# Two blocks of a transformer on one core: expert weights through seven and nine buffers in order of use, with the loops over experts written out

## The reference, cut to what matters

```python
def hier_moe(h, wr_g, br_g, wr_e, br_e, w_gate, w_up, w_down):
    p_group = softmax(xf @ wr_g + br_g)            # 4 groups, the best one is taken
    e_val, e_sel = top_k(fine of that group, 2)    # 2 of its 8 experts per token
    gate = p_top * softmax(e_val)
    ...
    y = (silu(x_rows @ w_gate[e]) * (x_rows @ w_up[e])) @ w_down[e]   # for each expert's tokens
    out[token] += y * gate
# layer 0 of the second block: conv_mixers, then hier_moe
# layer 1 of the second block: attn_mixers, then hier_moe, then the final rmsnorm
```

## Time and profile before

| what | value |
|---|---|
| runs | 2086.3, 2087.37, 2092.24 us; median 2087.37 |
| profiled execution | 2085.26 us, of which the span is 2083.3 us |
| TensorE busy | 2004.8 us (96%) |
| VectorE busy | 898.7 us (43%) |
| ScalarE busy | 371.7 us (18%) |
| moved by DMA | 592.64 MB, mean 284 GB/s |
| first expert stage | about 916 to 1390 us of the span |
| second expert stage | about 1598 to 2073 us |

### The profile page before, as it was taken

One profiled execution on the slowest core, in us unless ns is written; L12 is line 12 of the kernel. 1 busy time (PEld: TensorE's weight loads), 2 busy tenths in 40 slices (PEclk: granted clock), 3 DMA queues, 4 the chain that ended last, 5 costly groups with the idle time before them and its releaser, 6 DMA issues.

```text
span 2083.3 us, 21716 instructions
## 1 busy us (share of the span) xinstructions
PE 2004.8 (96%) x8126; PEld 1105.4 (53%) x8126; DVE 898.7 (43%) x1829; ACT 371.7 (18%) x767; POOL 93.0 (4%) x185
## 2 busy tenths in 40 slices
PE   8989999998999999799999999989999999999997
PEld 5556666545666658554443444447765443444442
DVE  3354553245355417856776666662534111011102
ACT  2321000033100010121111111112332111111111
POOL 1111110011111000000000000000000000000000
PEclk9999999999999999999999999999998999999999
DMA  7326885333488742529999999983251999999995
GB/s 265 139 81 245 300 326 222 135 122 121 157 317 313 273 162 81 202 80 416 430 428 429 428 429 428 428 321 122 81 202 41 408 427 428 428 429 428 428 428 249
DMA packets 109523, 592.64 MB, mean 284 GB/s; under 512 B 16663, under 2 KB 21270, under 8 KB 84886
## 3 DMA queue, kind: packets, MB, share of 16 engines
q1 hardware_dynamic: 96406, 541.48, 64.4%
q0 software_dynamic: 13056, 50.33, 6.4%
HBM read 590.74 MB, written 1.05 MB: 284 GB/s over the span
## 4 chain that ended last, share of the span: by engine, by line
PE 81%; DMA 12%; DVE 3%; POOL 1%; issue 1%; ACT 1%; SPq 0%; POOLq 0%; DVEq 0%; ACTq 0%
PE bank L1100 23%; DMA ring<-in_moe_w_up 12%; PE bank L758 11%; PE bank L771 11%; PE bank L982 7%; PE bank L694 6%; PE bank L1084 6%; PE bank L1091 3%; PE bank L895 3%; PE bank L1002 3%; PE bank L806 1%; PE bank L1215 1%; PE bank L1233 1%; PE bank L1262 1%; POOL rstd L619 1%
## 5 line engine op out<-in xcount | busy, mean ns | idle before, releaser
L1100 PE MATMUL bank<-ring,work 128*64 128x512 f32 x3072 | 672.9, 594 | 16.3 <-DMA ring<-in_moe_w_up 16.3
L1100 PEld LDWEIGHTS bank<-ring,work 128*64 128x64 f32 x3072 | 221.3, 137 | 436.2 <-issue 435.7
L2391 DVE SCALAR_TENSOR_TENSOR work<-work 128x512 f32<-128x512 f32 x384 | 258.6, 746 | 5.1 <-DVE work L2388 4.9
L758 PE MATMUL bank<-hT,ring 128*128 128x256 f32 x1024 | 223.5, 380 | 0.7 <-ACT hT L1373 0.7
L771 PE MATMUL bank<-ring,work 128*128 128x512 f32 x512 | 222.5, 593 | 0.0
L758 PEld LDWEIGHTS bank<-hT,ring 128*128 128x128 f32 x1024 | 194.8, 190 | 32.2 <-issue 6.9
L2395 DVE SCALAR_TENSOR_TENSOR work<-work,bank 128x512 f32<-128x512 f32 x32 | 21.9, 686 | 391.8 <-ACT work L1570 391.8
L2120 DVE SCALAR_TENSOR_TENSOR work<-ring,cond,work 128x512 f32<-128x512 f32 x168 | 126.3, 752 | 85.8 <-DMA ring<-in_ada_w 80.5
L771 PEld LDWEIGHTS bank<-ring,work 128*128 128x128 f32 x512 | 97.4, 190 | 115.4 <-issue 114.6
L982 PE MATMUL bank<-hT,ring 128*128 128x256 f32 x608 | 137.3, 388 | 0.3 <-ACT hT L1487 0.3
L694 PE MATMUL bank<-ring,hT 128*128 128x512 f32 (+1 forms) x320 | 135.0, 579 | 0.0
(11 more groups left out here) (384 smaller groups left out, 1517.6 us busy)
## 6 DMA issues: line engine op xcount, KB each, us to landing
ring<-in_moe_w_gate SPq DMA_DIRECT2D x64, 2048.0 KB, 15.4
ring<-in_moe_w_up SPq DMA_DIRECT2D x64, 2048.0 KB, 17.1
ring<-in_moe_w_down SPq DMA_DIRECT2D x64, 2048.0 KB, 12.7
ring<-in_ada_w POOLq DMA_DIRECT2D x48, 1024.0 KB, 9.3
ring<-in_w_up SPq DMA_DIRECT2D x16, 2048.0 KB, 12.8
ring<-in_w_down SPq DMA_DIRECT2D x16, 2048.0 KB, 10.0
ring<-in_w_in SPq DMA_DIRECT2D x10, 2048.0 KB, 8.0
ring<-in_cd_w_in SPq DMA_DIRECT2D x6, 2048.0 KB, 9.1
```

Source lines behind the costliest of these rows:

```text
L758: last = pe.matmul(B(4 + b)[:, (c % 2) * S:(c % 2) * S + S], w[:, k, c * P:c * P + P], hT[:, k, :], start=(k == 0), stop=(k == DT - 1))
L1100: last = pe.matmul(b[h, :], x[:, k, h], w[e][:, k, c0:c0 + 512], start=(k == 0), stop=(k == kk - 1))
L2391: mo.do(dve.scalar_tensor_tensor(fl(bias[:, h]), mask_b, rbt[:, bass.ds(12 * bk + h, 1)], fl(bias[:, h]), ALU.mult, ALU.add))
```

## The change

- **Memory.** A tile `seventh` of one slot is added. It takes the place of small tiles that only the first block and the preparation of the second use (masks, tables, row constants): they are now cut out of it, and it is free for weights in the expert stages. The router's bias gets a tile of its own.
- **Slots.** The first stage uses seven slots (six of `ring` and `seventh`), the second nine: also `work[:, 0:4096]`, which holds bias of the first eight heads, and one in two parts, `work[:, 4096:6144]` and `hT`. So the two-part slot is loaded by two DMAs.
- **Order.** The 96 matrices of a pass are numbered in order of use: gate, gate, up, up, down, down of each pair. Unit j goes to slot `RING_OF[i][j % 7]` (or 9), as soon as unit j-7 (or j-9) has been used.
- **Written out.** SP's loop over pairs and TensorE's loop over quads become straight code, each wait with its own value; the loop over passes stays.
- **Around it.** The attention stage's four first loads follow the unit that last held their slot; behind them the first matrix of stage 2 is loaded. More matrices are loaded before stage 2: after `gate1b` (slot on the bias), and after the router's logits (slot with `hT`). The products that clear the banks read `xres` and not `hT`. The final gain's load waits for the last down products.
- `landed2` now reuses the first block's semaphores, with `base2` added to the values.

```diff
+        seventh = sb("seventh", [P, UNIT])
...
+        def first_only(n, parts=P):
+            end7[0] += n
+            assert end7[0] <= UNIT, end7[0]
+            return seventh[0:parts, end7[0] - n:end7[0]]
...
+        brow = sb("brow", [P, 36])[:, :]
...
-        landed2 = [sem(f"landed2_{i}") for i in range(6)]
+        landed2 = landed + [sem("landed5")]
...
+        whole = lambda ap: [ap]
+        SLOT = [whole(ring[:, j, :]) for j in range(6)] + [whole(seventh[:, :]), whole(work[:, 0:UNIT]),
+                                                           [work[:, UNIT:UNIT + 2048], hT[:, :, :].rearrange("p k s -> p (k s)")]]
+        RING_OF = ((1, 2, 3, 4, 6, 5, 0), (6, 1, 2, 4, 5, 7, 3, 0, 8))
+        UNITS = 6 * (NE // 2)
+        USES = [[sum(RING_OF[i][j % len(RING_OF[i])] == z for j in range(UNITS)) for z in range(9)] for i in range(L2)]
+
+        def slot_of(i, j):
+            return RING_OF[i][j % len(RING_OF[i])]
...
+        def unit_landed(i, j, q, n0):
+            z = slot_of(i, j)
+            nth = sum(slot_of(i, x) == z for x in range(j + 1))
+            runs = USES[0][z] * q + nth if i == 0 else USES[0][z] * n0 + USES[1][z] * q + nth
+            return landedM[z], 16 * len(SLOT[z]) * runs
+
+        def unit_used(j, pairs):
+            kind = j % 6 // 2
+            return ("g_filled", "u_filled", "y_filled")[kind], (pairs + j // 6) * (1, 1, 2)[kind] + (2, 2, 4)[kind]
...
-            def moe_pairs(i, it0, first):
...
-                with sp.Fori(first, PAIRS) as pr:
-                    it = it0 + pr
-                    for kind, (name, value) in enumerate((("g_filled", it + 1), ("u_filled", it + 1), ("y_filled", 2 * it + 2))):
-                        sp.wait_ge(m[name], value)
-                        stand(sp, s["passed"])
-                        for e in range(2):
-                            moe_load(i, 2 * pr + e, kind, 3 * e + kind)
+            def moe_units(i, pairs, j0):
+
+                ahead = len(RING_OF[i])
+                for j in range(j0, UNITS):
+                    if j >= ahead:
+                        name, value = unit_used(j - ahead, pairs)
+                        sp.wait_ge(sM[name], value)
+                        stand(sp, s["passed"])
+                    moe_load(i, j)
...
-            moe_first(0, (3, 1, 4, 2))
+            moe_first(0, range(5))
             sp.wait_ge(s2["out_filled"], 1)
             moe_first(0, (5,))
             sp.wait_ge(s2["out_half"], 4)
-            moe_first(0, (0,))
+            moe_first(0, (6,))
...
-                    name, value = (("g_filled", 1), ("u_filled", 1), ("y_filled", 2), ("g_filled", 1))[j]
-                    sp.wait_ge(sM[name], value * PAIRS * n0 + value)
+                    last = max(x for x in range(UNITS) if slot_of(0, x) == j)
+                    name, value = unit_used(last, PAIRS * (n0 - 1))
+                    sp.wait_ge(sM[name], value)
...
+                if j == CD_RING - 1:
+                    sp.wait_ge(sM["y_filled"], 2 * PAIRS * n0 + 2)
+                    moe_first(1, (0,))
             sp.wait_ge(s2["job_filled"], JOB2["vd1"] + 1)
             moe_first(1, (1, 2))
             sp.wait_ge(s2["scores"], 16)
-            moe_first(1, (4, 5))
+            moe_first(1, (3, 4))
+            sp.wait_ge(s2["masked"], 16)
+            stand(sp, s["passed"])
+            sp.wait_ge(s2["job_filled"], JOB2["gate1b"] + 1)
+            moe_first(1, (5,))
             sp.wait_ge(s2["out_filled"], 2)
-            moe_first(1, (3,))
+            moe_first(1, (6,))
             sp.wait_ge(s2["out_half"], 8)
-            moe_first(1, (0,))
-            moe_stream(1, n0)
+            moe_first(1, (7,))
+            sp.wait_ge(sM["logits_ps"], 2)
+            moe_first(1, (8,))
+            n1 = moe_stream(1, n0)
+            sp.wait_ge(sM["y_filled"], 2 * PAIRS * (n0 + n1) + 2)
...
-                        pe.matmul(B(b), zeros, hT[:, 0:2, :].rearrange("p k s -> p (k s)"), start=True, stop=True, skip_group_check=True)
+                        pe.matmul(B(b), zeros, xres[:, 0, 0:512], start=True, stop=True, skip_group_check=True)
...
-                    with pe.Fori(0, QUADS - 1) as qd:
-                        quad((q + before) * QUADS + qd, True)
-                    quad((q + before) * QUADS + QUADS - 1, False)
+                    for qd in range(QUADS):
+                        quad(q, it0 + qd, qd)
```

More of the change, by code:

```diff
@@ L365, in first_and_second_block @@
             "rel_used", "scores", "masked", "exp_done", "pt_filled", "pt_drained", "x_half", "cd_ready", "od_filled", "lam_exp", "o_ready", "final_in", "moe_small_in")}
-        landed2 = [sem(f"landed2_{i}") for i in range(6)]
+        landed2 = landed + [sem("landed5")]
+        base2 = [16 * L1 * (UNITS1 // RING1 + (1 if r == U_LORA % RING1 else 0)) for r in range(RING1)] + [0]
         landed3 = [sem(f"landed3_{i}") for i in range(CD_RING)]
@@ L523, in moe_stream @@
                     with sp.Fori(1, n) as q:
-                        moe_pairs(i, (q + before) * PAIRS, 0)
+                        sp.wait_ge(m["y_filled"], 2 * PAIRS * (q + before) + 2)
+                        stand(sp, s["passed"])
+                        moe_units(i, (q + before) * PAIRS, 0)
                 return n
@@ L997, in out_part @@
                 j = j0 + u
[L998 removed]
+                pe.wait_ge(landed_of[j % slots], (base2[j % slots] if landed_of is landed2 else 0) + 16 * (j // slots + 1))
                 w = wide2(j, 1024, 4, slots)
@@ L1094, in scatter, with product, units_landed, hidden @@
                             last.then_inc(m["last_scatter"], 1)
-                def product(b, x, w, k, kk, c0):
+                def product(b, x, j, k, kk, c0):
                     for e in range(2):
                         h = slice(SLOTS * e, SLOTS * e + SLOTS)
-                        last = pe.matmul(b[h, :], x[:, k, h], w[e][:, k, c0:c0 + 512], start=(k == 0), stop=(k == kk - 1))
+                        last = pe.matmul(b[h, :], x[:, k, h], rows_of(i, j + e, k)[:, c0:c0 + 512], start=(k == 0), stop=(k == kk - 1))
                     return last
-                def hidden(it, j):
-                    pr = 2 * it + j
+                def units_landed(j, q):
+                    for e in range(2):
+                        pe.wait_ge(*unit_landed(i, j + e, q, before))
+                def hidden(q, it, qd, j):
+                    pr, unit = 2 * it + j, 12 * qd + 6 * j
                     x = xeT[:, :, P * j:P * j + P]
@@ L1113, in hidden @@
                                 pe.wait_ge(m["xt_drained"], 4 * it + 1 + k // 2)
-                            last = product(b, x, (wslot[c], wslot[c + 3]), k, DT, 0)
+                            last = product(b, x, unit + 2 * c, k, DT, 0)
                         last.then_inc(m[name], 1)
@@ L1126, in hidden_turned, with down, quad @@
                     last.then_inc(m["at_filled"], 1)
-                def down(pr, hf):
+                def down(q, pr, unit, hf):
                     if hf == 0:
                         pe.wait_ge(m["at_drained"], pr + 1)
-                        for c in (2, 5):
-                            pe.wait_ge(landedM[c], 16 * pr + 16)
+                        units_landed(unit + 4, q)
                     for k in range(4):
-                        last = product((G, U)[hf], aTe, (wslot[2], wslot[5]), k, 4, 512 * hf)
+                        last = product((G, U)[hf], aTe, unit + 4, k, 4, 512 * hf)
                     last.then_inc(m["y_filled"], 1)
-                def quad(it, more):
+                def quad(q, it, qd):
+                    more = qd < QUADS - 1
                     for j in range(2):
-                        pr = 2 * it + j
-                        hidden(it, j)
+                        pr, unit = 2 * it + j, 12 * qd + 6 * j
+                        hidden(q, it, qd, j)
                         pe.wait_ge(m["pg_drained"], pr + 1)
@@ L1148, in quad @@
                         gates_turned(it, j)
-                        down(pr, 0)
+                        down(q, pr, unit, 0)
                         if more and j == 1:
@@ L1158, in quad @@
                             gather(3, T)
-                        down(pr, 1)
+                        down(q, pr, unit, 1)
                 with pe.Fori(0, n) as q:
```

64 lines of the change are left out of this document (30 added, 34 removed).

## The result

| | before | after |
|---|---|---|
| median of 4 runs each, taken side by side | 2086.84 us | 2072.39 us |
| all runs | 2086.18 to 2092.24 | 2069.73 to 2073.28 |
| profiled execution (its span) | 2085.26 (2083.3) | 2069.73 (2067.7) |

The ratio is 0.9916, with a 95% interval of 0.9899 to 0.9932. The medians are 14.45 us apart; 14.05 were forecast.

What follows compares the result with a forecast made beforehand. In the expert stages the weight DMA was taken as slightly slower than TensorE, 1.33 us lacking per four experts. Terms -4.89 - 9.76 + 0.6 = -14.05 gave 2071.2 profiled, 2073.3 us median; range 2067.5 to 2080.5.

Steps and rivals of the forecast that it cites:

- The stalls as the reserve (19.43 us): Both expert stages: TensorE's waits for weights lose 9.67 and 9.76 us, the most a deeper ring can give inside them.
- Stage 2, gain 9.76, with 4.92 us to spare: Second expert stage: three more slots land weights 14.68 us earlier, ending all 9.76 us of stall, with 4.92 left.
- Stage 1, 4.89 for a slot: First expert stage: one more slot lands weights 4.89 us earlier; 4.78 us of stall stay.
- Code, +0.6 (0 to 1.3): Straight code's fetches delay a DMA engine in stage 1: 0.6 us taken, 1.3 if one engine is hit twice.
- A DMA queue full from the first product on: Expert stages, both kernels: queue full from the first gate product, so landings move by what was loaded ahead, 4.89 per matrix.
- the rival of 2097.0: Code fetches pile up on one DMA engine, 14.5 us behind by a stage's end; slower, 2097.0 us, chance 0.06.
- Branches hidden, 0: TensorE's loop: the 14 branches back, 0.208 us each, lie hidden in the x80 groups, so removing them gains 0.
- The final gain, 0: Final gain loaded after the last down product, still landing before its reader at 2076.94: cost 0, at worst 1 us.
- One slot's worth only: Rival: stage 2 gains only 4.89 like stage 1, its late slots counting for nothing; 2078.2 us, chance 0.10.
- All stalls gone: Rival: the ring also fills queue gaps near a stage's start, no stall left in stage 1; 2068.0 us, chance 0.10.
- branches not hidden: Rival: the loop's 14 branches cost open time, so 2.9 us more come back; 2070.4 us, chance 0.02.
- Given back: Rival: open register sums (6.1), late final gain (1) and one engine's two fetches return most gain; 2081.1 us, chance 0.10.

Runs made afterwards that it cites:

- code_more: Changed kernel plus two semaphore increments, on which nothing waits, after each expert-stage product on TensorE: 2073.75 us, ratio 0.9922 to the kernel before.
- head_half: Changed kernel with the first half of stage 1's unit 7 loaded ahead once into half of hT: 2073.54 us, ratio 0.9915 to the kernel before.
- seven_seven: Changed kernel with seven slots in stage 2 too, in place of nine: 2078.03 us, ratio 0.9936 to the kernel before.

## Why the prediction was right, step by step

- **The stalls as the reserve (19.43 us).** Right. The starts of equal rows gave 9.67 and 9.76 to win, and stage 2 gave 9.70 and stopped at 451.6, with TensorE the bound.
- **Stage 2, gain 9.76, with 4.92 us to spare.** Right for after. The spare was smaller than 4.92: with eight slots it should have been nothing and the stage at 451.6, and it was 453.85. So nine slots leave under 2.7 us (4.89 - 2.2) of it. The trace of after has 2.27: by so much the last pair's up matrices land before their products.
- **Stage 1, 4.89 for a slot.** The sum came out 3.17 with everything in it, 4.29 foreseen. That the split into 4.89 for the slot and 0.6 for the code held even roughly is luck: with the code written out in both, the seventh slot was worth 7.8 to 11.1, and writing out cost 4.2 to 7.9 with six slots. The two act on each other, which the prediction's sum did not allow for. No run has seven slots with the loops kept, so what each is worth there is a subtraction.
- **Code, +0.6 (0 to 1.3).** This is the term that was mis-sized. In after 6.50 us of stall are left in stage 1 (408.30 less seven times 57.40), where 9.67 - 4.89 = 4.78 would be by the slot alone: 1.7 and not 0.6, outside the bounds given (0 and 1.3). The mechanism was right: landings of 18.93 to 20.33 us just where q8 runs, code_more with six blocks more and 1.6 us more, and a stage with spare depth that pays nothing. What was too low is the step "the slowest is late by one fetch, as now": at the last landing waited for, the slowest engine is 3.69 us behind the first where it was 1.89 before, 1.8 more, since some engines are hit again. The prediction's own sign of a pile-up, a period above 59 us, shows once, 59.99 us, and only in part does it mean what it was to prove: the rival of 2097.0 has twelve more blocks at 1.21 us each on one engine, 14.5, where 1.7 showed.
- **A DMA queue full from the first product on.** Not quite. Near 980 us it has a gap in before as in after, and by the landings on both sides of it that is what made head_half worthless. It is as long in both kernels (391 and 392 GB/s), so it did no harm to the sum.
- **Branches hidden, 0.** Right: the x80 group takes 17.34 us with the branch and in stage 1 of after 17.34 without it (1149.58); the x96 groups stayed at 20.75. The Trainium skill (Runtime: NRT & Kernel Launch, Instruction fetch mechanics) prefers unrolling because a taken branch may force a fetch. In this kernel the trace shows the reverse: the loop drew 3 blocks in 930 to 1370 us, the straight code 15, and with six slots the straight code is 4 to 5 us a stage slower. By the same section of the Trainium skill a block's crossing is mostly hidden; that holds for TensorE (stage 2 of code_more) and not for the weights beside it.
- **Register sums, 0.** Right: no gap shows in stage 2, where TensorE never stands.
- **Slots filled in time.** Right: no first product of stage 2 waits for a landing, and its first x64 group starts 226.22 us behind the last down products of stage 1, 227.89 before.
- **The final gain, 0.** Right: issued at 2053.4, landed 3.7 us later, and its reader starts at 2061.34, right behind DVE's own work and 4.2 us after the landing. The bound of 7.4 us was twice what it took.

```profile
L602 SPq DMA_DIRECT2D hT<-in_final_norm_g x1: 347/347/347, 2053.4 to 2053.4; - x1
...
DMA to landing us min/median/max: 3.7/3.7/3.7
```

- **The rivals.** One slot's worth only (2078.2) is what seven_seven is, at 2078.03, and not what the change is. All stalls gone (2068.0) falls with the 6.50 us left in stage 1, and branches not hidden (2070.4) with groups as long with a branch as without. Given back (2081.1) falls with the sums that show nowhere and the final gain that lands in time; only its third part, one engine hit twice (1.3 for 0.6), came about, with 1.7.
- **The total.** The terms gave -14.05; the stages moved by 12.87, and the medians by 14.45. The missing 1.2 us and the extra 1.6 us of parts that the change leaves as they were nearly cancel, which is luck within the scatter of a run.

## What to carry to other kernels

Where TensorE and a stream of weights are nearly in balance, count slots and not rates: a permanent slot is worth about a matrix's transfer time (4.0 us from seven to eight, 4.89 the transfer), and more where without it the queue runs short (7.8 to 11.1 from six to seven), until the other engine is the bound; a single early load is levelled at the first place where the queue is empty, and smaller loads can cost in rate what they give in depth. Written-out code is not free beside a saturated stream: here it delayed landings, not the engine that runs it, and cost most where there was no depth to absorb it. So test such a change together with the depth that it needs: here the same straight code was 0.5% slower with six slots and part of a 0.8% gain with seven and nine.

## What was not expected of the hardware

- A block of code of 16 KB and the row of weights behind it take 1.1 us each in place of 0.61, which costs one DMA engine some 1.5 us. The lag stays while the queue is full, and fifteen blocks spread the engines by 3.7 us. With six slots the stream runs short as well: 416 GB/s against 424 over 440 us, with 12 more blocks.
- Rows of 8 KB per partition moved at 421 GB/s, rows of 16 KB at 428 (1050 to 1090 us).
- The granted clock falls or doesn't at the same place of the same program (1.00 and 0.83 over 500 to 530 us), with 2.3 us between the starts of stage 1, which is as much as some of the terms above.
